# Channel-major projections: matmuls issued in runs of four of 512 columns and four of 256, in place of two and two

## What is computed

```
h    = rmsnorm(x, norm1_gain)
proj = h @ w_in                        # 2048 -> 7 groups of 1024 and 8 gates
o_a  = hgrn2_mixer(...)                # gated linear recurrence, 8 heads
o_b  = fox_mixer(...)                  # forgetting attention, 8 heads
x    = x + concat(o_a, o_b) @ w_out
h    = rmsnorm(x, norm2_gain)
x    = x + (silu(conv(h @ w_gate)) * (h @ w_up)) @ w_down     # 2048 -> 5632 -> 2048
x    = rmsnorm(x, final_norm_gain)

for i in (0, 1):                       # second block, two layers
    u = h @ w_in_2[i]                  # 2048 -> 2*1536 + 2*512
    branch = pooling (layer 0) or block attention (layer 1)
    mem_o  = memory_attention(mem_q, mem, w_mem_kv_2[i])
    y = concat(branch * silu(gate_b), mem_o * silu(gate_m)) @ w_out_2[i]
    h = layer_norm(ALPHA * h + y)
```

## Time and profile before

| what | value |
|---|---|
| median of 3 executions | 2025.08 us (2024.7 to 2025.14) |
| the profiled execution | 2025.91 us |
| its span, first to last instruction | 2024.2 us |
| TensorE busy | 1999.6 us, 99% of the span, 10731 matmuls |
| TensorE's weight loads | 1715.6 us, 85%, 10731 |
| VectorE, ScalarE busy | 1234.2 us (61%), 870.4 us (43%) |
| granted TensorE clock, mean | 0.997 of 2.4 GHz |
| HBM | 193 GB/s over the span |

### The profile page before, as it was taken

The page is one execution under the profiler, slowest core; times in us unless marked ns, Lnnn a source line. Parts: engine busy times, 40 slices in busy tenths (PEclk is TensorE's granted clock), DMA queues, the critical chain, the costliest instruction groups (busy, mean ns, idle before and its releaser), DMA issues.

```text
span 2024.2 us, 24661 instructions
## 1 busy us (share of the span) xinstructions
PE 1999.6 (99%) x10731; PEld 1715.6 (85%) x10731; DVE 1234.2 (61%) x1097; ACT 870.4 (43%) x814; POOL 21.2 (1%) x62
## 2 busy tenths in 40 slices
PE   7999999999999999999999999999999999999998
PEld 6888988888888888888888888888888888888886
DVE  5665556655666665456666545756865764566665
ACT  5444444444544443334444335334444534344542
POOL 2000000000000000000000000000000000000000
PEclk9999999999999999999999999999999999999999
DMA  9755455475655555565555755746495656554562
GB/s 329 232 181 177 135 167 167 146 271 172 212 186 189 188 186 187 189 206 187 187 192 182 271 198 198 232 154 187 148 355 186 218 188 195 182 159 149 194 199 87
DMA packets 295000, 393.22 MB, mean 194 GB/s; under 512 B 6414, under 2 KB 225355, under 8 KB 293227
## 3 DMA queue, kind: packets, MB, share of 16 engines
q1 hardware_dynamic: 292032, 365.19, 55.6%
q0 software_dynamic: 2400, 26.28, 3.3%
q10 hardware_dynamic: 459, 0.16, 0.0%
HBM read 383.22 MB, written 8.39 MB: 193 GB/s over the span
## 4 chain that ended last, share of the span: by engine, by line
PE 98%; DMA 1%; SPq 1%; DVE 1%; ACT 0%; issue 0%; DVEq 0%; ACTq 0%
PE G L385 39%; PE G L389 19%; PE G L432 11%; PE G L431 11%; PE G L430 11%; PE SB L699 1%; DMA xt<-in_x 1%; PE OB L720 1%; PE G L451 0%; PE G L450 0%; PE G L452 0%; PE OB L723 0%; PE SB L596 0%; PE TB L1010 0%; SPq L840 0%; PE OB L1024 0%
## 5 line engine op out<-in xcount | busy, mean ns | idle before, releaser
L352 DVE TENSOR_TENSOR hl_ring<-raw,hl_ring 128x2048 fp32r<-128x2048 f32 (+1 forms) x348 | 784.0, 2256 | 523.6 <-ACT hl_ring L349 523.3
L349 ACT ACTIVATE hl_ring<-raw 128x2048 fp32r<-128x2048 f32 (+1 forms) x348 | 655.2, 1886 | 592.8 <-PE G L432 311.1
L385 PE MATMUL G<-ahl,hl_ring 128*128 128x512 f32 x2112 | 665.2, 396 | 0.0
L389 PEld LDWEIGHTS G<-ahl,hl_ring 128*128 128x128 f32 x2112 | 396.7, 188 | 93.7
L389 PE MATMUL G<-ahl,hl_ring 128*128 128x256 f32 x2112 | 415.1, 278 | 0.0
L385 PE MATMUL G<-ops,hl_ring 128*128 128x512 f32 x1216 | 384.2, 397 | 0.0
L385 PEld LDWEIGHTS G<-ahl,hl_ring 128*128 128x128 f32 x2112 | 322.0, 189 | 0.8 <-issue 0.5
L389 PEld LDWEIGHTS G<-ops,hl_ring 128*128 128x128 f32 x1216 | 228.4, 188 | 53.9
L389 PE MATMUL G<-ops,hl_ring 128*128 128x256 f32 x1216 | 239.1, 278 | 0.0
L385 PEld LDWEIGHTS G<-ops,hl_ring 128*128 128x128 f32 x1216 | 185.6, 189 | 0.3
L430 PE MATMUL G<-hl_ring,hhl 128*128 128x512 f32 x352 | 136.9, 389 | 0.0
(11 more groups left out here) (338 smaller groups left out, 1724.9 us busy)
## 6 DMA issues: line engine op xcount, KB each, us to landing
raw<-in_w_in SPq DMA_DIRECT2D x120, 1024.0 KB, 5.4
raw<-in_w_out SPq DMA_DIRECT2D x48, 1024.0 KB, 5.2
raw<-in_w_ffn_gate SPq DMA_DIRECT2D x44, 1024.0 KB, 5.1
raw<-in_w_ffn_up SPq DMA_DIRECT2D x44, 1024.0 KB, 5.1
raw<-in_w_ffn_down SPq DMA_DIRECT2D x40, 1024.0 KB, 5.1
raw<-in_w_kv_shared SPq DMA_DIRECT2D x24, 1024.0 KB, 5.1
raw<-in_w_mem_kv SPq DMA_DIRECT2D x16, 1024.0 KB, 5.1
ahl<-memop_scratch POOLq DMA_DIRECT2D x2, 4096.0 KB, 14.6
```

The lines of the kernel that those rows point to most:

```text
L349: eng.activation(hi[:, s, 0:size], raw[:, r, 0:size], ACT.Copy).then_inc(hi_ready, 1)
L352: eng.tensor_tensor(lo[:, s, 0:size], raw[:, r, 0:size], hi[:, s, 0:size].bitcast(F32), ALU.subtract).then_inc(lo_ready, 1)
L385: eng.matmul(G[:, 2 * pair + b, :], hi[:, s, w], p.rhs(k), start=first and q == 0, stop=False)
L389: last = eng.matmul(G[:, 2 * pair + b, 0:TOK], lo[:, s, w], p.rhs(k)[:, 0, :], start=False, stop=final and q == len(ks) - 1)
```

## The change

In `alternate`, `order` is taken four entries at a time in place of two: both channel blocks of two k-blocks. First come their four matmuls of 512 columns, then their four of 256. The number of matmuls, loads, waits and semaphore updates is the same, and so are all operands; within a tile their order changes. The last matmul of a tile, which raises `tile_used`, is the same one.

```diff
-            for g in range(0, len(order), 2):
-                for (b, ks, width, col, first, final), q in order[g:g + 2]:
+            for g in range(0, len(order), 4):
+                for (b, ks, width, col, first, final), q in order[g:g + 4]:
                     kt, k = ks[q]
                     w = slice(kt * width + col, kt * width + col + P)
                     eng.matmul(G[:, 2 * pair + b, :], hi[:, s, w], p.rhs(k), start=first and q == 0, stop=False)
-                for (b, ks, width, col, first, final), q in order[g:g + 2]:
+                for (b, ks, width, col, first, final), q in order[g:g + 4]:
                     kt, k = ks[q]
                     w = slice(kt * width + col, kt * width + col + P)
                     last = eng.matmul(G[:, 2 * pair + b, 0:TOK], lo[:, s, w], p.rhs(k)[:, 0, :], start=False,
                                       stop=final and q == len(ks) - 1)
```

## The result

| | before | after |
|---|---|---|
| median of 6 executions each | 2025.01 us (2024.31 to 2025.15) | 2032.08 us (2031.66 to 2033.15) |
| ratio, with its 95% interval | | 1.0037 [1.0027, 1.0047] |
| span of the profiled execution | 2024.2 us | 2030.1 us |

A forecast was written before the change was run, and what follows sets the result against it. The prediction took TensorE, busy 1999.6 of 2024.2 us, to bound the kernel. A gain of 4.9 ns on each of 848 eights gave 4.2 us, so 2025.08 - 4.2 = 2020.9 us, with a range of 2016.5 to 2029.

The forecast's parts named there:

- What bounds the kernel: Whole kernel: TensorE, busy 1999.6 of 2024.2 us; other engines wait for it, so each nanosecond per matmul reaches the end whole.
- The pitch now and the three neighbours: Form A at 1393.3 ns an eight; unmixed streams at 226.7 (512 columns) and 120.0 (256); pairs in turn at 353.3.
- a loss for each change of size that falls as runs get longer: Form A's matmuls: fixed pace per size plus 6.7 ns a back and forth in singles, 3.3 in twos; gain 4.2 us.
- halved again it is 1.7 ns: Loss for the one back and forth left in an eight; gain 4.9 ns x 848 = 4.2 us.
- My upper bound for that term: The last back and forth in an eight costs at most 6.7 ns, as between singles: 1393.4 ns, no gain.
- That form A's 512s take 233 ns and form F's 227: Pitch from 512 to 512, 233 ns in form A and 226.7 in form F; cited against a pitch set by pairs alone.
- 7 ns of waiting inside the engine, taken over from the matmuls of 256: Form A's 512s, recorded at 396 ns against 389 in form F; a wait that a longer run wouldn't repeat.
- No change: Form A: each transition between matmuls keeps today's price, 1394 ns an eight, +0.6 us, 2025.7 us; chance 24%.
- The slower rival: Form A: 256s fall to 120 ns, 512s stay at 233.3 (two banks); 1409.4 ns an eight, +13.7 us, 2038.8; chance 15%.
- Its threshold: The slower rival decides from a 256-to-256 pitch of 114.6 ns with the 512s unchanged; 0.2% of loss at 116.2.
- the prediction's own sign of being wrong: In the profile after: 256s over 116 ns with 512s at 233, new idle before L385, or pitch moving outside form A.
- The much faster rival: Form A: 512s reach 226.7 ns, 256s keep 115; 1374.6 ns an eight, -15.9 us, 2009.2; chance 9%.

## Why the prediction was wrong, step by step

**What bounds the kernel** was right. The loss in pitch came out at the end whole: 6.9 us by the starts in form A, 7.1 us in the medians. The two profiled spans differ by 5.9, as the one of after waited 1.4 us less for its first weight tiles. That no wait and no other engine would answer was right too.

**The pitch now and the three neighbours** have the right paces. One count is wrong: the 59.16 us in form F hold 87 rounds of three matmuls, so 261 matmuls and not 87 in 29 rounds; the pace of 226.7 came out right, as it was taken from the round of 0.68 us. The settled paces of 226.7 and 120.0 are confirmed by the runs of eight and sixteen. But the forget gate's 353.3 ns a pair, which gave the 6.7 ns for singles, is one of two paces that singles have: at the other, 346.7, they lose nothing.

**The step that failed is the model, "a loss for each change of size that falls as runs get longer", and with it the term "halved again it is 1.7 ns".** It was drawn through two points, 6.7 ns for singles and 3.3 for twos, and the first of them depends on the phase (0 or 6.7). Measured in fours is 16.7 ns for the one cycle that is left in an eight, where two cycles of 3.3 had been: 10.0 ns more an eight, times 848 is 8.5 us if every tile were undisturbed, and 6.9 us as they are. My upper bound for that term, 6.7 ns, was the worst value that I had seen, and no reason excluded a higher one. Singles and twos could not show it: a run of two ends before the dear start of the 512s has run its course, and all its 256s are in their cheap start. Twos pay 13 ns a cycle in the 512s and get 10 back in the 256s. Fours pay for a dear start four matmuls long (234.2, 234.6, 232.1 and 228.3 ns, 22 in all), and their 256s take 117.5, 119.6, 118.8 and 118.3, so only 6 ns are given back. Eight and sixteen pay 27 and get back 7 to 8, but once or twice a tile.

**That form A's 512s take 233 ns and form F's 227** stood in the text, as did the guess that they carry "7 ns of waiting inside the engine, taken over from the matmuls of 256". The first part of that guess agrees with the traces, in which a matmul's end is modelled: in the runs of sixteen a 512 is recorded at 396 to 397 ns while its pitch is 233 to 236, and at 389 once it is 227. The second, "which a longer run wouldn't repeat", is what failed: it lasts five matmuls and not two.

**No change** (24%) failed because a pitch depends on more than the matmul and the one behind it. It had 1394 for 1403.3 measured: the first three 512s did stay at 232 to 235, but it gave all 256s their cheap 115, and from 256 to 256 it took 117.5 to 119.6.

**The slower rival** (15%) had the sign and most of the picture. It forecast 512s at 233.3 and 256s at 120; measured are 232.3 and 118.5, and 1403.3 ns an eight stands between its 1409.4 and today's. Its threshold, 256s above 114.6 with the 512s unchanged, was passed, and so was the prediction's own sign of being wrong, 256s over 116 with the 512s at 233. But its cause was wrong: the two banks have no part in it, and the run of four of 256 is free when the run of 512 stays at two (933.3 ns), so the 256s are not dear for the length of their own run. It was also oversized, 13.7 us for 7.1.

**The much faster rival** (9%) failed: no settled stream of 256 columns went under 120, and in the fours the 512s took 232.3 for its 226.7 and the 256s 118.5 for its 115.

**The range** was too narrow above. It left out nearly all of the slower rival, though that rival's 120 ns was a pace that the trace held over 99 matmuls.

**What stays open** is the inside of the engine: why a 512 behind 256s is dear for five matmuls, and what the state is that a matmul of 64 + 192 columns changed in four phases, where 128 + 128, 192 + 64 and 248 + 8, tried in one phase each, did not. The runs show that there is such a state; they don't show what it is. No run changed the weight loads, so what part they have in either is not shown. Nor is it explained which pace a phase starts with in the runs of one. The four whole phases at 5653.3 come behind form F, and those at 5546.7 behind small matmuls or a phase that had that pace; but the undisturbed tiles of in_fq come behind small matmuls too and run at the dear pace.

## What to carry to other kernels

In a stream that mixes matmul sizes, take the loss of a whole cycle of the pattern against the settled paces of its sizes, and don't draw a line from two short patterns to a longer one: here one, two, four, eight and sixteen cost 0 or 6.7, 3.3, 16.7, 20 and 20 ns a cycle. Regrouping changes a few parts in a thousand either way and costs one run to try; if long runs are wanted, make them much longer than the five matmuls that settling takes, or stay at two. A bound taken from the worst case yet seen is no bound if the new case lets something run longer than any seen.

## What was not expected of the hardware

- In the runs of eight and sixteen a matmul of 512 columns with its own weights behind a run of 256s has a pitch of 233, 236, 228, 232 and 231 ns before it settles at 226.7; one of 256 behind 512s starts at 113 and 119 before 120. Behind four of 512 the first of 256 takes 117.5.
- The same stream can hold two paces for hundreds of matmuls: singles at 346.7 or 353.3 ns a pair. One of 256 columns split into 64 + 192 in a phase's first tile decided it in four phases. Runs of sixteen with 488 columns went at 220.0 or 225.7 each, in turn.
- Once settled, 504 columns cost as much as 512 and 264 as much as 256, and from 240 columns down to 192 the pitch stays at 112 ns.
- Which bank is written, and whether neighbours share the moving operand, made no difference of a nanosecond.
